# Spreading the modulation steps beside the weight units by a share per matrix

## The reference, cut to what matters

```python
m = (sc_c @ w_mod[l] + b_mod[l])[:, None, :]        # 1024 -> 6 * 1024, l = 0, 1
sh1, s1, g1, sh2, s2, g2 = jnp.split(m, 6, axis=-1)
h = modulate(rmsnorm(x, norm_g[l, 0]), sh1, s1)
...                                                 # l = 0: y, yc = even_mixer(h, hc, ...); l = 1: y = conv(h)
x = x + g1 * y
x = x + g2 * sq_relu_mlp(modulate(rmsnorm(x, norm_g[l, 1]), sh2, s2), w_ff1[l], w_ff2[l])
```

## Time and profile before

| | |
|---|---|
| Median of three runs | 1627.76 us |
| The profiled execution | 1628.15 us, of which span 1626.9 us |
| TensorE busy | 1394.3 us, 86% |
| VectorE busy | 1215.1 us, 75% |
| ScalarE busy | 728.9 us, 45% |
| Mean granted TensorE clock | 0.958 of full |
| Read from memory | 474.75 MB, 292 GB/s |

### The profile page before, as it was taken

The page is one execution under the profiler, slowest core; times in us unless marked ns, Lnnn a source line. Parts: engine busy times, 40 slices in busy tenths (PEclk is TensorE's granted clock), DMA queues, the critical chain, the costliest instruction groups (busy, mean ns, idle before and its releaser), DMA issues.

```text
span 1626.9 us, 20640 instructions
## 1 busy us (share of the span) xinstructions
PE 1394.3 (86%) x7504; PEld 1034.0 (64%) x7504; DVE 1215.1 (75%) x2373; ACT 728.9 (45%) x1636; POOL 354.3 (22%) x321
## 2 busy tenths in 40 slices
PE   7899789999898899998999779997787777777776
PEld 2778679999887899997878766543232222222222
DVE  7866688887897688886866687877777787777654
ACT  3545355554566655554344444444333343333322
POOL 5100010000000100003001124464444444444430
PEclk9999799999999999998999889999999999999999
DMA  9653259998530389894523359999999999999995
GB/s 376 264 204 119 104 186 348 330 341 326 200 108 1 126 319 341 332 339 150 181 105 104 117 226 392 420 419 420 420 420 421 420 421 420 421 419 421 420 421 213
DMA packets 66055, 477.15 MB, mean 293 GB/s; under 512 B 7329, under 2 KB 7329, under 8 KB 8737
## 3 DMA queue, kind: packets, MB, share of 16 engines
q0 software_dynamic: 36864, 268.45, 39.8%
q1 hardware_dynamic: 28944, 206.32, 34.4%
q10 hardware_dynamic: 146, 1.06, 0.2%
HBM read 474.75 MB, written 1.05 MB: 292 GB/s over the span
## 4 chain that ended last, share of the span: by engine, by line
PE 47%; DMA 26%; DVE 17%; ACT 5%; issue 3%; POOL 2%; POOLq 0%; ACTq 0%; DVEq 0%
DMA row_h<-in_uv,crow 21%; PE ps L1969 8%; PE ps L1578 6%; PE ps L1579 5%; PE ps L1580 5%; DMA row_x<-in_uv,crow 5%; DVE HID L807 4%; PE ps L1855 4%; PE ps L1854 4%; PE ps L1852 4%; DVE WB L473 3%; ACT WB L1096 1%; PE ps L1597 1%; PE ps L1618 1%; DVE row_h L1030 1%
## 5 line engine op out<-in xcount | busy, mean ns | idle before, releaser
L473 DVE TENSOR_TENSOR WB<-ring,WB 128x1024 fp32r<-128x1024 f32 x232 | 287.8, 1241 | 99.1 <-ACT WB L1096 95.9
L1096 ACT ACTIVATE WB<-ring 128x1024 fp32r<-128x1024 f32 x232 | 243.4, 1051 | 128.6 <-PE ps L1855 85.1
L1969 PE MATMUL ps<-ring,P 128*128 128x512 f32 x448 | 214.1, 622 | 68.5 <-ACT P L1421 68.4
L1578 PE MATMUL ps<-hH,WB 128*128 128x256 f32 x920 | 268.7, 292 | 4.5 <-DVE WB L473 2.9
L1579 PE MATMUL ps<-hL,WB 128*128 128x256 f32 x920 | 261.9, 285 | 0.0
L1580 PE MATMUL ps<-hH,WB 128*128 128x256 f32 x920 | 261.8, 285 | 0.0
L1969 PEld LDWEIGHTS ps<-ring,P 128*128 128x128 f32 x448 | 84.2, 197 | 192.4 <-ACT P L1421 104.9
L1411 ACT ACTIVATE On<-On 128x2 f32<-128x2 f32 x128 | 26.0, 203 | 378.6 <-DVE On L1030 378.5
L1030 DVE CUSTOM_DVE_ANT_0 ring<-ring,cT 128x1024 f32<-128x1024 f32 x112 | 136.4, 1226 | 79.0 <-DMA ring<-in_uv,crow 77.8
L1578 PEld LDWEIGHTS ps<-hH,WB 128*128 128x128 f32 x920 | 178.1, 194 | 9.6 <-issue 4.9
L1579 PEld LDWEIGHTS ps<-hL,WB 128*128 128x128 f32 x920 | 178.2, 194 | 2.2 <-issue 2.2
(11 more groups left out here) (297 smaller groups left out, 2777.2 us busy)
## 6 DMA issues: line engine op xcount, KB each, us to landing
ring<-in_stream SPq DMA_DIRECT2D x116, 1024.0 KB, 6.0
ring<-in_um SPq DMA_DIRECT2D x66, 1024.0 KB, 7.2
ring<-in_wm SPq DMA_DIRECT2D x4, 1024.0 KB, 15.6
bias<-in_bias SPq DMA_DIRECT2D x2, 2048.0 KB, 14.9
HID<-in_um SPq DMA_DIRECT2D x4, 512.0 KB, 12.7
ring<-in_uv,crow POOLq DMA_INDIRECT x112, 28.4
xT<-in_xT ACTq DMA_DIRECT2D x1, 1024.0 KB, 7.9
cT<-in_cxT SPq DMA_DIRECT2D x1, 1024.0 KB, 7.8
```

The costliest lines, as they stand in the source:

```text
L473: ve.tensor_tensor(unit_dst(j, 1), unit_src(j), f(unit_dst(j, 0)), ALU.subtract).then_inc(s_lo, 1)
L1096: se.activation(unit_dst(j, 0), unit_src(j), ACT.Copy).then_inc(s_hi, 1)
L1578: te.matmul(o, wh[:, c], hi[:, kt, :], start=(kt == 0), stop=False)
L1969: mm = te.matmul(ps[4 + 2 * n + q][:, :], diag[:, g % 8, :], row_ap[row_of[g]][:, 1024 + q * 512:1536 + q * 512], start=(g % 128 == 0), st ...
```

## The change

The table `beside` is no longer given by hand. Each matrix has a share, the mean number of steps beside one of its units; the shares are summed up over the units, and a unit gets as many whole steps as have come together, at most two. Four stretches of five units each, around the ends of sublayers, and the first four units get none; what would have fallen there stays in the sum and comes out after. The assertion that the table holds NM steps is gone; `mods` returns when all are done, so that entries past the 128th step have no effect.

```diff
@@ -356,17 +356,15 @@
         NM = 8 * len(mod_cgs)
         mod_g = {x: g for g, x in enumerate(mod_cgs)}
 
-        beside = [0] * NU
-        for u, n in enumerate((2, 2, 2, 2, 1, 1, 1, 1, 1, 1)):
-            beside[4 + u] = n
-        for u, n in enumerate((2, 2, 2, 2, 2)):
-            beside[first["w_out", 0] + u] = n
-        for l in range(2):
-            for k in range(48):
-                beside[first[f"ff1_{l}", 0] + 4 + k * 7 // 6] = 1
-        for u in range(4):
-            beside[first["w_in2", 0] + u] = 2
-        assert sum(beside) == NM
+        share = {"w_in": 1.6, "w_out": 0.9, "ff1_0": 0.7, "ff2_0": 0.7, "pw2": 1, "ff1_1": 0.6, "ff2_1": 0.6,
+                 "w_in2": 0.9, "w_out2": 0.9, "wq": 0.9}
+        ends = [first["ff1_0", 0], first["pw1", 0], first["ff1_1", 0], first["w_in2", 6]]
+        beside, left_over = [], 0.0
+        for i, (name, b, kind, u) in enumerate(units):
+            quiet = i < 4 or any(e - 3 <= i <= e + 1 for e in ends)
+            left_over += share.get(name, 0)
+            beside.append(0 if quiet or name not in share else min(2, int(left_over + 1e-9)))
+            left_over -= beside[-1]
         emptying = []
 
         xsrc = {"x0": xT, "ctx": cT, "mlp0": xT, "conv": xT, "ln": yc, "mlp1": xT, "fin": xT, "b2": xT, "ffn": xT}
```

## The result

The changed kernel takes 1656.09 us (median of 4 timed runs, 1650.22 to 1661.84) where the kernel before takes 1627.84: a ratio of 1.017, with a 95% interval of 1.0149 to 1.0191. It is slower. The forecast was 1648 with 1634 to 1662; the direction and the range held, and the likeliest value was 8 us low; the measured median lies nearer to the 1660 of the rival in which the clock falls as well. The profiled execution took 1654.66 us (span 1653.4), 26.5 us more than the one of before.

A forecast was written before the change was run, and what follows sets the result against it. The prediction saw the heads bound by a round of three engines, with TensorE and VectorE in balance at one step. Its sum, 1628.15 + 10.0 + 6.5 + 4.9 - 1.4 = 1648.2, became 1647.8 against the median; range 1634 to 1662.

The forecast's parts named there:

- The heads: Units 8 to 19, 18 steps more: 14.6 us later, 2.0 of it at the entry; bounds 7 and 21.8 + 0.8.
- w_out: Six steps fewer at w_out: 4.6 us gained, 2.5 of it at the L644 of 183.06; bounds 2.5 and 7.3.
- The bursts in the feed-forwards: Two, two, two steps at each feed-forward's start: 2.7 us lost in the first, 3.8 in the second, 6.5 together.
- pw2: Eight steps where none were: 4.9 us later from VectorE's time and late weights; bounds 1.5 and 7.
- w_in2: Eight steps fewer: 1.4 us gained, what TensorE waits for VectorE there; bounds 0 and 2.5.
- Hidden: Rival: VectorE's idle time takes up all added steps, and removals at w_out and w_in2 are gained; 1622, chance 5%.
- Only the heads: Rival: feed-forward and pw2 bursts cost nothing; only heads, w_out and w_in2 count; 1636, chance 15%.
- The clock falls as well: Rival: new TensorE waits lower its clock, up to 9 us at pw2 and feed-forwards, some 3 in heads; 1660, 20%.

The follow-up runs named there:

- x_ff_resident: Kernel before plus 2, 2, 1 additional step-sized VectorE instructions without transfers beside units 30 to 32 and 118 to 120; 1628.29 us, ratio 1.0007.
- x_ff: Kernel before with 2, 2, 2, 1, 1, 0 steps at the third to eighth unit of both feed-forwards, four fewer late in each; 1638.41 us, ratio 1.006.
- x_pw2: Kernel before with 2, 2, 2, 1, 1 steps in pw2, beginning with a whole weight pair, taken from the second feed-forward; 1629.51 us, ratio 1.0009.
- x_pw2_odd: As x_pw2, but one step moved from the second feed-forward to the first, so pw2 begins mid-pair; 1634.9 us, ratio 1.0048 against the kernel before.
- x_win2: Kernel before with the 8 steps of w_in2 moved into the gaps of both feed-forwards; 1625.45 us, ratio 0.9985.
- x_pw2_even: Kernel before with 8 steps in pw2, one beside each unit, taken from the second feed-forward; 1627.19 us, ratio 0.9997.
- x_best: Kernel before with second steps in the heads only beside units 9, 13, 17, fewer at w_out, w_in2's 8 in the feed-forwards; 1621.58 us, ratio 0.9969.
- x_pw2_resident: Kernel before plus 8 additional step-sized VectorE instructions (2, 2, 2, 1, 1) beside pw2, without transfers; 1634.23 us, ratio 1.0038.

## Why the prediction held, and where it was short

**The heads: the rounds right, the start wrong.** For the nine heads from L644 at 104.33 to that at 159.87 the sum said 68.1 us; the changed kernel took 68.05 (110.10 to 178.15). Three of the nine rounds took 6.52 or 6.53 us and six, with a gate piece, a copy or the Gelu in them, 7.79 to 8.40. What was short is the entry: the forecast had the first of these heads 2.0 late, and it came 5.8 late. Of the 3.8 missing, 0.8 were there before any moved step: the last pair ahead of unit 8 came in at 84.25, against 83.45 before. The other 3.0 are the clock behind the wait at unit 8, 1.0 in the first scores (2.56 us from TensorE's start to L642, against 1.61) and 2.0 in the round that follows (9.04 against 7.01). The step beside unit 8 was costed at 0.8, by the copy's delay alone. The rival on the clock had just this, some 3 us in the long units of the heads; the likeliest value left it out.

**`w_out`: right.** 4.6 forecast; the lateness shrinks from 18.3 at the last L642 of the gate's heads to 12.75, so 5.5. The parts were less well placed: at the last head's L642 (199.96, before 183.06) only 1.4 are gained where 2.5 were forecast, and the rest comes after it.

**The bursts in the feed-forwards: right in kind, short in size.** 6.5 forecast, 10.2 measured. VectorE's part, forecast with 1.6 of TensorE's waits at each place, is 1.1 by x_ff_resident, and the transfers are the larger part, as the working had it. What was mis-sized is the transfer's landing (the step waits 2.2 us for the pair in the changed kernel and 3.2 in x_ff, where the working had 1.1) and the clock, which the term left out. In the changed kernel TensorE's waits are 3.2 and 4.3 us, 7.5 of the 10.2; behind the second burst, from 606 to 612 us, it was granted 0.72, an estimate of 1.7 us more (6 x 0.28), and behind the first 1.00.

**`pw2`: right in kind, short by the clock.** 4.9 forecast, 7.75 measured; 39.6 - 35.0 = 4.6 in x_pw2, where the clock stays up in `pw2`. By the table of the experiments the 7.75 are 4.4 of new waits and 4.6 of longer busy products, most of it the clock, less 1.3 ahead of `pw2`, where the convolution's last 48 products took 7.28 us instead of 8.55 (granted 0.87 against 0.76). The term left the clock out. The working also took a step as 1.21 us, and four of them are recorded with 1.75 or 1.76 instead of 1.28, each with GpSimd's L1476 beside it; what this adds lies inside the 4.4 of waits and is not parted from them. And it doesn't reckon with the burst's beginning in the middle of a pair (81 steps are done before it); x_pw2 and x_pw2_odd show what that is worth.

**`w_in2`: right in direction, the size open.** The occupancy of VectorE, 14 of 16 us, was no measure of what 8 steps less would bring, and the wait of 1.4 us was near it: 1.9 in x_win2. The 3.5 of the changed kernel can't be put down to the table. From the reciprocal at the end of the second feed-forward (744.59 before) to the one at 926.84, single executions took 178.9 to 179.5 us in the four kernels without steps at `w_in2` and 177.5 to 186.3 in the nine with them.

**The rivals.** *Hidden* fell by the rounds of 6.53 us. *Only the heads* fell by x_ff and x_pw2_odd. *The clock falls as well* was right in the mechanism: in the profiled execution the clock fell in the first head, behind the second burst and twice in `pw2`, by the numbers above some 3, 1.7 and 3 us. (TensorE's busy time over the whole span rose by 8.7 with the same products.) The forecast kept it apart as a case of its own, 1660, but it is no case, it is a spread. Beside the three batches of experiments the kernel before ran between 1625.2 and 1631.9; the changed kernel ran 39 times in all between 1650.2 and 1661.8, and its mean granted clock goes with the time: 0.949 in the two executions of mean 1660.5, 0.954 in eight of mean 1654.6, 0.957 in two of mean 1651.1 (correlation -0.70). An estimate from these: 0.88 us for each 0.001 of the mean clock. That the clock makes the spread is not shown by a correlation, but it fits. The forecast should have put an expected part of it, some 6 to 8 us, on the likeliest value; that the wider range took the measured time in was owed to this rival's share of it. That execution by execution the same wait can end either way is in the two profiles at one place, outside of the change. TensorE waits 1.19 us before one and 1.18 before the other for the output of the second attention, and then the granted clock differs. The kernel before, TensorE in order of time:

```profile
871.66 0.66 PE L1716 MATMUL ps<-ident,On 128*128 128x128 f32 x4 [1.19 <-DVE On L623]
```

the 6 us there, columns as in the earlier trace rows:

```profile
870.00:876.00 6.00, 4.81 (x27) 4.05 (x27) 4.57 (x9) 3.34 (x10) 0.00 (x0) 0.82 0.51 176
```

The changed kernel, the same two views:

```profile
900.39 0.66 PE L1714 MATMUL ps<-ident,On 128*128 128x128 f32 x4 [1.18 <-DVE On L621]
```

```profile
899.00:905.00 6.00, 4.83 (x35) 4.07 (x35) 4.58 (x9) 3.62 (x11) 0.00 (x0) 1.00 0.48 176
```

The clock is 0.82 in the first and 1.00 in the second. The wait of 1.89 us at the start of `pw2` says the same: full speed behind it in the kernel before, 0.92 over the next 20 us in x_pw2_even. The working read the one good case as evidence against this rival.

## What to carry to other kernels

When idle time lies inside a round of several engines, add the work to the round, not to the idle time: by occupancy the heads had 19 us of room on VectorE, by the round none. Spread filler work by what each unit's slowest engine leaves, one piece at a time, and remember the buffer behind it: with two pairs of weights in flight a burst of three pairs waits for a transfer, and more so when it starts in the middle of a pair. Price a new wait of TensorE with the clock that it may cost, and as a spread rather than as a separate case. When two profiles differ by a few microseconds, compare a point ahead of the change first, and the busy time of the same products: here the first took 1.3 us off x_best's gain at `w_out`, and the second showed that x_pw2_even's loss is mostly the clock.

## What the runs showed of the hardware

A VectorE step with two operands in the on-chip buffer slows down when it begins beside GpSimd. In the thirteen kernels, up to 960 us, 34 of the 1664 steps were recorded with 1.75 to 1.78 us, and each of them began while GpSimd was in an addition of 0.9 to 1.2 us; of the steps at 1.27 to 1.29 us none overlapped one. The cost is 0.48 us a step. So did four of the eight additional instructions of x_pw2_resident, which read rows that lie in the chip all along (1.75 or 1.76 against 1.22 or 1.23 us). The Trainium skill ("GPSIMD Engine Reference", Specifications) says that GpSimd shares its SBUF interfaces with VectorE and contends with instructions that have two SBUF inputs; the trace agrees for an instruction that begins second. The low parts have two such inputs too, and the 182 of them in which GpSimd's addition began only after they had (up to 830 us) kept their 1.20 to 1.22 us.

TensorE's clock fell after some waits of 1.2 to 1.9 us and not after others, in the same program and in kernels that are alike up to there. Behind the wait of 1.89 us before `pw2` the next 148 products took 18.39 us at 1.00 in the kernel before and 20.32 us at 0.92 in x_pw2_even.
